# Row factor one step later, four padded buffers, and the neighbourhood and retention tiles scaled by VectorE as it empties their bank

## The reference, cut to what matters

```
h = rms_norm(x, pre_mix_g[l])              # x * row_factor(token) * gain(column)
z = h @ w_in[l]                            # 2048 -> 57 tiles of 128 columns
za, zb, zc = jnp.split(z, [NA_IN_COLS, NA_IN_COLS + RW_IN_COLS], axis=-1)
ya = neighbourhood_attention(...za...)     # 12 tiles
yb = rwkv7_mixer(zb, ...)                  # 21 tiles, token_shift first
yc = retention_mixer(...zc...)             # 24 tiles
x = x + rms_norm(jnp.concatenate([ya, yb, yc], -1) @ w_out[l], post_mix_g[l])
u = jnp.square(jax.nn.relu(rms_norm(x, pre_mlp_g[l]) @ w_up[l])) @ w_down[l]
x = x + rms_norm(u, post_mlp_g[l])
```

## Time and profile before

| | |
|---|---|
| median of 3 runs | 1336.45 us (1335.89 to 1338.19) |
| profiled execution | 1339.37 us, span 1337.6 us, granted clock 0.992 |
| PE busy | 1300.4 us, 97% of the span |
| DVE, ACT, POOL busy | 841.8, 645.5, 329.9 us |
| HBM traffic | 222.56 MB read, 2.10 MB written |

### The profile page before, as it was taken

The page is one execution under the profiler, slowest core; times in us unless marked ns, Lnnn a source line. Parts: engine busy times, 40 slices in busy tenths (PEclk is TensorE's granted clock), DMA queues, the critical chain, the costliest instruction groups (busy, mean ns, idle before and its releaser), DMA issues.

```text
span 1337.6 us, 24793 instructions
## 1 busy us (share of the span) xinstructions
PE 1300.4 (97%) x10204; PEld 1127.1 (84%) x10204; DVE 841.8 (63%) x1151; ACT 645.5 (48%) x991; POOL 329.9 (25%) x273
## 2 busy tenths in 40 slices
PE   9898999999999999999999999999999999999997
PEld 8686888888889898888888888888888888888886
DVE  8767787777775987556555555555554554555564
ACT  7464555565434446457444444444444444444453
POOL 0123234352316231000445555555530000000000
PEclk9899999999999999999999999999999999999999
DMA  9555433223339344782866666666656555565672
GB/s 307 145 159 150 126 106 97 81 81 98 106 107 226 95 127 130 276 274 77 232 181 198 190 188 191 189 190 189 189 189 194 196 194 190 193 197 191 191 235 93
DMA packets 281857, 226.28 MB, mean 169 GB/s; under 512 B 15184, under 2 KB 259024, under 8 KB 281104
## 3 DMA queue, kind: packets, MB, share of 16 engines
q1 hardware_dynamic: 281360, 223.44, 55.4%
q0 software_dynamic: 240, 1.18, 0.3%
q10 hardware_dynamic: 144, 0.07, 0.0%
HBM read 222.56 MB, written 2.10 MB: 168 GB/s over the span
## 4 chain that ended last, share of the span: by engine, by line
PE 65%; DVE 4%; ACT 2%; DMA 2%; issue 1%; DVEq 0%; ACTq 0%
PE psum L2336 30%; PE psum L1917 17%; PE psum L1928 9%; PE psum L1901 2%; PE psum L1907 2%; PE psum L1902 2%; DMA raw<-in_w_out 2%; DVE w_lo L895 1%; ACT w_hi L1490 1%; PE psum L2393 0%; PE psum L2312 0%; DVE arena L1398 0%; PE psum L2214 0%; PE psum L2304 0%; PE psum L2099 0%
## 5 line engine op out<-in xcount | busy, mean ns | idle before, releaser
L895 DVE TENSOR_TENSOR w_lo<-raw,w_hi 128x1024 fp32r<-128x1024 f32 x394 | 500.2, 1272 | 373.7 <-ACT w_hi L1490 370.4
L1490 ACT ACTIVATE w_hi<-raw 128x1024 fp32r<-128x1024 f32 x394 | 417.9, 1064 | 428.4 <-PE psum L2336 186.9
L1917 PE MATMUL psum<-act_both,w_hi 128*128 128x512 f32 x1296 | 319.7, 395 | 9.9 <-ACT w_hi L1490 9.8
L2336 PE MATMUL psum<-w_hi,act_both 128*128 128x512 f32 x1216 | 327.8, 390 | 1.4 <-DVE arena L1319 0.9
L1917 PEld LDWEIGHTS psum<-act_both,w_hi 128*128 128x128 f32 x1296 | 239.3, 190 | 57.3 <-ACT w_hi L1490 10.9
L2336 PEld LDWEIGHTS psum<-w_hi,act_both 128*128 128x128 f32 x1216 | 227.9, 188 | 49.9 <-issue 1.2
L2336 PE MATMUL psum<-w_lo,act_both 128*128 128x512 f32 x608 | 187.6, 389 | 0.0
L1928 PEld LDWEIGHTS psum<-act_both,w_lo 128*128 128x128 f32 x1296 | 170.4, 192 | 8.2 <-DVE w_lo L895 0.3
L1928 PE MATMUL psum<-act_both,w_lo 128*128 128x256 f32 x1296 | 174.2, 283 | 0.0
L1901 PE MATMUL psum<-act_both,w_hi 128*128 128x256 f32 x576 | 157.8, 305 | 0.2 <-ACT w_hi L1490 0.2
L1902 PE MATMUL psum<-act_both,w_hi 128*128 128x256 f32 x576 | 145.7, 284 | 0.0
(11 more groups left out here) (246 smaller groups left out, 1149.8 us busy)
## 6 DMA issues: line engine op xcount, KB each, us to landing
raw<-in_w_up SPq DMA_DIRECT2D x128, 512.0 KB, 4.0
raw<-in_w_down SPq DMA_DIRECT2D x128, 512.0 KB, 3.9
raw<-in_w_in SPq DMA_DIRECT2D x114, 512.0 KB, 4.1
raw<-in_w_out SPq DMA_DIRECT2D x32, 512.0 KB, 4.9
arena<-in_x_t SPq DMA_DIRECT2D x4, 512.0 KB, 7.6
arena<-in_na_rpb SPq DMA_DIRECT2D x16, 128.0 KB, 4.5
arena<-in_x SPq DMA_DIRECT2D x1, 2048.0 KB, 8.7
out_x<-arena SPq DMA_DIRECT2D x3, 512.0 KB, 2.7
```

What stands on the lines that cost most here:

```text
L895: dve.tensor_tensor(by_half(h, low(h)), by_pair(h, raw[:, place[h] % RAW]), by_half(h, high(h)).bitcast(F32), ALU.subtract).then_inc(s["lo ...
L1490: act.activation(by_half(h, high(h)), by_pair(h, raw[:, place[h] % RAW]), ACT.Copy).then_inc(s["hi_half"], 1)
L1917: last = pe.matmul(bank[b], w_hi[:, h % SPLIT, at:at + P], act_both[:, kt].rearrange("p a t -> p (a t)"), start=kt == 0, stop=stop and kt ...
L2336: last = pe.matmul(bank[4 * t + 2 * j + b], lhs[:, tokens], w[:, b * 512:(b + 1) * 512], start=start, stop=stop)
```

## The change

- The gap of the row sum goes from 10 to 11, and root and reciprocal follow at the gaps 12 and 13. The squares of x are added by three 1024-wide additions, one of 512 and one of 256, in place of five reductions; each addition inside the first loop comes one block earlier.
- Four padded buffers in place of two, and larger lags for sum, scale, `to_zs` and shift; the first drains are spread over one gap each. The first turn's preparation starts later, in fewer gaps.
- DVE's `scaled_nr` empties all 18 neighbourhood and retention groups. ACT's `to_nr`, POOL's `scale_na` and POOL's multiplication of the two tables are gone, and what waited for them waits for the drain.

```diff
-SUM_LAG, SCALE_LAG, ZS_LAG, SHIFT_LAG = 3, 4, 9, 13
+SUM_LAG, SCALE_LAG, ZS_LAG, SHIFT_LAG = 11, 12, 20, 28
-NORM_GAP = 10
-ZS_FROM, SHIFT_FROM = 8 * NORM_GAP + 9, 8 * NORM_GAP + 17
+NORM_GAP = 11
+ZS_FROM, SHIFT_FROM = 8 * (NORM_GAP + 5), 8 * (NORM_GAP + 6)
+PADS = 4
...
-        PE_STARTS = {15: "root", 19: "lora"}
-        STARTS = {12: "square", 17: "root", 18: "factor", 20: "norm", 21: "lora", 26: "sums_0", 29: "keys_0",
-                  31: "sums_1", 33: "keys_1"}
+        PE_STARTS = {21: "root", 24: "lora"}
+        STARTS = {19: "square", 22: "root", 23: "factor", 25: "norm", 26: "lora", 29: "sums_0", 32: "keys_0",
+                  34: "sums_1", 36: "keys_1"}
...
-            def scale_na(i):
-
-                pool.wait_ge(s["bank_free"], RW_GROUPS + i + 1)
-                z = cut(nr_at(2 * i), 2, T)
-                pool.tensor_tensor(z, z, row_scale.unsqueeze(1).broadcast_to([P, 2, T]), ALU.mult).then_inc(
-                    s["na_scaled"], 1)
-                pool.wait_ge(s["na_scaled"], i + 1)
...
-            pool.tensor_tensor(turns, turns, row_scale.unsqueeze(1).broadcast_to([P, 2, T]), ALU.mult).then_inc(
-                s["table_scaled"], 1)
...
-                dve.tensor_reduce(x_part[:, q], x_sq[:, q].rearrange("p (k t) -> p t k", t=T), AX_X, ALU.add).then_inc(
-                    s["x_parted"], 1)
+                if q > 1:
+                    dve.wait_ge(s["x_added"], q - 1)
+                dve.tensor_tensor(x_sq[:, 0], x_sq[:, 0], x_sq[:, q], ALU.add).then_inc(s["x_added"], 1)
...
-                dve.tensor_reduce(x_total, x_part.rearrange("p q t -> p t q"), AX_X, ALU.add).then_inc(
-                    s["x_totalled"], 1)
+                dve.wait_ge(s["x_added"], KT // BLOCK_KT - 1)
+                dve.tensor_tensor(x_sq[:, 1, 0:2 * T], x_sq[:, 0, 0:2 * T], x_sq[:, 0, 2 * T:4 * T], ALU.add).then_inc(
+                    s["x_added"], 1)
+                dve.wait_ge(s["x_added"], KT // BLOCK_KT)
+                dve.tensor_tensor(x_total, x_sq[:, 1, 0:T], x_sq[:, 1, T:2 * T], ALU.add).then_inc(s["x_totalled"], 1)
...
                 if q >= 2:
-                    add_squares(q - 2)
+                    add_squares(q - 1)
...
-            at = {"gap": 0, "lo": BLOCK_H, "shift": 0, "sum": 0, "nr": SCALED_FROM}
+            at = {"gap": 0, "lo": BLOCK_H, "shift": 0, "sum": 0, "nr": RW_GROUPS}
...
-                if at["gap"] in (NORM_GAP - 2, NORM_GAP - 1):
-                    add_squares(at["gap"] - NORM_GAP + 4)
-                if at["gap"] == NORM_GAP - 1:
+                if at["gap"] == NORM_GAP - 3:
+                    add_squares(KT // BLOCK_KT - 1)
+                if at["gap"] == NORM_GAP - 2:
                     total_squares()
...
-            def to_nr(g):
-                tiles = group_tiles(g)
-                j = tiles[0] - RW_T
-                act.wait_ge(s["gemm_half"], 2 * (tiles[-1] + 1))
-                if j + 1 >= ZPAD_TILE:
-                    act.wait_ge(s["pad_free"], 2 + RW_GROUPS)
-                act.activation(cut(nr_at(j), 2 * T), bank[6 + g % 2], ACT.Copy).then_inc(s["bank_free"], 1)
...
-                if g < RW_GROUPS:
-                    return max(complete(g) + ZS_LAG, ZS_FROM)
-                return complete(g) + DRAIN_LAG
+                return max(complete(g) + ZS_LAG, ZS_FROM + 8 * g)
...
-            scaled(pe)
+            drained(pe, NA_T - 1)
```

More of the change, by code:

```diff
@@ L715, in tilde @@
                 return [first, nothing, bonus_and_queries, lambda: key_rate(1), nothing, lambda: queries(1), nothing]
-            at = {"gap": 0, "scale": 0, "na": 0}
+            at = {"gap": 0, "scale": 0}
             def scale_z(g):
@@ L855, in _ @@
             dve.memset(eps, EPS).then_inc(s["eps_set"], 1)
-            dve.memset(zpad[:, 0], 0.0).then_inc(s["pad_free"], 1)
-            dve.memset(zpad[:, 1], 0.0).then_inc(s["pad_free"], 1)
+            for n in range(PADS):
+                dve.memset(zpad[:, n], 0.0).then_inc(s["pad_free"], 1)
             dve.memset(all_ones, 1.0).then_inc(s["ones_set"], 1)
@@ L937, in shift @@
                         z = z_of(ct)
[L938 removed]
+                        last = dve.scalar_tensor_tensor(z, zpad[:, g % PADS, j, at:at + T], vect(mu)[:, ct:ct + 1], z,
                                                         ALU.mult, ALU.add)
@@ L944, in shift @@
                 last.then_inc(s["pad_free"], 1)
-            at = {"gap": 0, "lo": BLOCK_H, "shift": 0, "sum": 0, "nr": SCALED_FROM}
+            at = {"gap": 0, "lo": BLOCK_H, "shift": 0, "sum": 0, "nr": RW_GROUPS}
             def gap():
                 done = DONE[at["gap"]]
-                while at["shift"] < RW_GROUPS and max(complete(at["shift"]) + SHIFT_LAG, SHIFT_FROM) <= done:
+                while at["shift"] < RW_GROUPS and max(complete(at["shift"]) + SHIFT_LAG, SHIFT_FROM + 8 * at["shift"]) <= done:
                     shift(at["shift"])
@@ L1506, in to_zs @@
                     ct = RW_ORDER[n]
-                    last = act.activation(z_of(ct), zpad[:, g % 2, j, 1:T + 1], ACT.Copy, scale=small[:, 64 + ct:65 + ct])
+                    last = act.activation(z_of(ct), zpad[:, g % PADS, j, 1:T + 1], ACT.Copy, scale=small[:, 64 + ct:65 + ct])
                 last.then_inc(s["bank_free"], 1)
@@ L1513, in copy_z @@
                 act.wait_ge(s["pad_free"], g + 1)
-                act.activation(zpad[:, g % 2, 0:len(group_tiles(g)), 1:T + 1], rw_halves(g)[:, :, 1], ACT.Copy).then_inc(
+                act.activation(zpad[:, g % PADS, 0:len(group_tiles(g)), 1:T + 1], rw_halves(g)[:, :, 1], ACT.Copy).then_inc(
                     s["z_copied"], 1)
-            def to_nr(g):
-                tiles = group_tiles(g)
-                j = tiles[0] - RW_T
-                act.wait_ge(s["gemm_half"], 2 * (tiles[-1] + 1))
-                if j + 1 >= ZPAD_TILE:
-                    act.wait_ge(s["pad_free"], 2 + RW_GROUPS)
-                act.activation(cut(nr_at(j), 2 * T), bank[6 + g % 2], ACT.Copy).then_inc(s["bank_free"], 1)
             at = {"gap": 0, "hi": BLOCK_H, "copy": 0, "drain": 0}
             def drain_due(g):
-                if g < RW_GROUPS:
-                    return max(complete(g) + ZS_LAG, ZS_FROM)
-                return complete(g) + DRAIN_LAG
+                return max(complete(g) + ZS_LAG, ZS_FROM + 8 * g)
             def gap():
                 done = DONE[at["gap"]]
-                while at["drain"] < SCALED_FROM and drain_due(at["drain"]) <= done:
-                    if at["drain"] < RW_GROUPS:
-                        to_zs(at["drain"])
-                    else:
-                        to_nr(at["drain"])
+                while at["drain"] < RW_GROUPS and drain_due(at["drain"]) <= done:
+                    to_zs(at["drain"])
                     at["drain"] += 1
@@ L1547, in gap @@
                     at["hi"] += 1
-                if at["gap"] == NORM_GAP - 2:
+                if at["gap"] == NORM_GAP - 3:
                     squares(KT // BLOCK_KT - 1)
-                if at["gap"] == NORM_GAP:
+                if at["gap"] == NORM_GAP + 1:
                     row_root()
@@ L1780, in _ @@
                 turn(i)
-            assert at["hi"] == OUT_H + 2 and at["drain"] == SCALED_FROM and at["gap"] == len(DONE) - 1
+            assert at["hi"] == OUT_H + 2 and at["drain"] == RW_GROUPS and at["gap"] == len(DONE) - 1
             gate_heads(RET_CT - 2, RET_CT)
```

40 lines of the change are left out of this document (16 added, 24 removed).

## The result

| | before | changed |
|---|---|---|
| median | 1336.17 us (1333.13 to 1338.19, 4 runs) | 1326.54 us (1324.87 to 1327.22, 4 runs) |
| ratio | | 0.9925, 95% interval 0.9906 to 0.9945 |
| profiled execution | 1339.37 us | 1326.27 us, span 1324.4, granted clock 0.996 |

What follows compares the result with a forecast made beforehand. PE bounds the kernel, busy 97%, so only its idle time and slow stretches can be won. Terms -7.1 - 1.9 - 1.2 + 0 = -10.2 us, from 1336.45 to 1326.2 us; range 1317.5 to 1335.5, own case 1321 to 1331.

Steps and rivals of the forecast that it cites:

- Row sum and first sums: Dense stage: the 2.1 us wait ahead of the row sum moves to half 8; booked 0.
- Behind the row factor: Dense stage, halves behind the row sum: ACT no longer waits for POOL ahead of conversions; -7.1 us, bounds 0 and 7.1.
- for the median I take 1336.45 - 10.2: Final step: the summed gain of 10.2 us subtracted from the median of the runs, giving 1326.2 us.
- Keys: First turn's `keys_0`, `sums_1`, `keys_1` in the dense stage: 6.4 us lost where 8.3 were; -1.9 us.
- First products: Group 9's shifts now stand behind the DVE piece PE waits for, ahead of the first level; -1.2 us, bounds 0 and 2.
- Drains: Product stage: 12 more DVE drains, +2 us uncovered, against -2 for POOL's six multiplications gone; 0, bounds +8.2 and -4.
- the bound of -4: Lower bound of the drains' term in the product stage: at most 4 us won.
- The 1.25 us wait: Wait at 250.98 in the product stage, right behind a POOL multiplication; cited for booking -2 us for POOL's absence.
- PE's waits for DVE in the product stage: Sign that the forecast is right: these waits stay as large as before; doubled would show the second rival.
- the second rival: DVE becomes the product stage's bound, each drain reaching PE in full: 1334.4 us, chance 0.13.

Runs made afterwards that it cites:

- The earlier sum: Changed kernel with only the sums of groups 0 and 9 one gap earlier on DVE: 1323.77 us, ratio 0.9914.
- the drains alone: Kernel before with only DVE's drains of all 18 groups, without the later row factor and the four buffers: 1330.45 us, ratio 0.9965.
- the two edits of the kernel before: Kernel before with ACT's square moved from gap 12 to 16: 1336.03 us; the same with four padded buffers in place of two: 1335.14 us.
- a second drain: Changed kernel with each of the first 12 DVE drains done twice: 1330.62 us, ratio 0.9960.
- the copied drains: Changed kernel with ACT's `to_nr`, POOL's `scale_na` and POOL's table multiplications put back: 1332.21 us, ratio 0.9975.

## Why the prediction was right in sum and wrong in its terms

- *Row sum and first sums, 0.* The mechanism was right, the wait stands at half 8 with 1.84 us for the 2.1 forecast. The booked 0 left out that half 8 then runs slowly: half 11 starts at 43.65 against 42.26, +1.4 us. The earlier sum takes both away.
- *Behind the row factor, -7.1.* That PE waits nowhere there is right: every half from 12 to 20 takes the undisturbed 2.79 us. Between the two profiles the three halves took 15.44 and 8.38 us, so -7.1 to the digit. The step that failed is "for the median I take 1336.45 - 10.2": the loss was measured in one execution that lay 2.9 us above the median, and then subtracted in full from the median. The three other executions with the same order or nearly so lost less; each is one profile. From half 8 to half 16 it was 32.93 us there, 30.57 with the drains alone, 30.25 and 30.30 in the two edits of the kernel before, and 26.71 now. The term with that of the row sum is about -3.7 (26.71 less the mean of the three), not -6.2. The cause named was incomplete too: ACT's 4.30 us for POOL alone costs some 2 to 3; what held up the conversions was a row of pieces (scaling, square, copy, sum behind the shifts). In two edits one of them took over when the one ahead of it went; no run takes all of them away one by one, so their shares stay open.
- *Keys, -1.9.* Right: -2.6, with waits of 0.38, 2.56 and 0.18 us at the halves 34, 36 and 40, where 1.2 and 3.2 were forecast at 34 and 36 and 2.0, hidden, at 38. Against the profile with the drains alone (37.60) it is -1.2.
- *Not booked, +2.1.* With the longer lag the sum of group 9 falls behind DVE's first products, and PE, which needs its bank, waits 1.99 us at 141.63. The prediction looked at the sum of group 0 alone; the same lag moved ten others.
- *First products, -1.2.* Right: from the first matmul behind the dense stage (148.37 before, 141.63 now) to the first products 5.78 and 4.69 us, -1.1. In the turn that follows +1.0 came back: the shift of the last group now stands ahead of a DVE result that PE needs, and PE waits 0.37 and 1.29 us (for L1100 and L1085) where it waited 0.77 once.
- *Drains, 0.* This term hid the most. It booked +2 for uncovered drains and -2 for POOL's absence. The measured sum is -5.2 on the kernel before and -5.4 on the changed one (-4.7 and -6.1 by the ratios), beyond the bound of -4, though the interval of the former, -2.5 to -6.7, reaches it; POOL's six multiplications alone are 4.4 to 5.9. The 1.25 us wait of the earlier trace rows was read as the price of such a collision. Its price was that wait, a second one 27 us later (1.23 at 278.22) and the clock behind them: that turn's mean was 0.93 and it took 47.18 us in place of 42.81. PE's waits for DVE in the product stage, which were to stay as large, fell: those of 0.2 us or more between 147 and 430 us from 6.8 to 4.6 us.

So two errors of about the same size, with opposite signs, met, and that the sum is right is luck: 10.2 us were booked for the parts outside the drains, which by the medians bring about 4 (9.6 in all less the drains' 5.2 to 5.4), some 6 too much, and the drains were booked some 5 too low. The advice of the Trainium skill (Perfetto Trace Analysis, Optimizing Scalar/DVE Operations) that a saturated DVE may be relieved by giving work to ACT, by which the second rival would have been the forecast, did not decide here: a second drain costs PE about half its length, but the first one came with the removal of POOL's multiplications, which is worth more.

## What to carry to other kernels

Ask of an instruction not only what it costs on its own engine but whom it slows while it runs: 12 drains on the busier engine won time because six multiplications on an engine that is three quarters idle stood beside results that PE waits for. Size a stall in more than one execution, or take it off that execution alone: in the third turn the waits came back to 0.1 us with the copied drains (1.25 and 1.23 us, then 1.26 and 1.24), but what the clock cost behind them did not (47.18 us, then 44.53). And when a lag is changed for all groups, look at each place where another engine needs the result: both new waits for sums sat at the groups 0 and 9, behind the block phase and behind half 41, and giving those two their old lag, with group 9's scale and two steps of the preparation moved by a gap, was worth as much again as the whole change.

## What the runs showed that was not expected

Behind waits of the same kind the eight matmuls of half 14 took 3.78 us in the kernel before (idle 3.57) but 2.11 with the drains alone (idle 2.87), where the eight of half 10 had taken 3.26 instead of 2.19. The order is the same; which half pays for a low clock, and for how long, was not the same. Why is left open. Also left open is how much a drain costs PE by itself, since doing it twice measures the second one, and why the executions of the kernel before scatter by 7 to 8 us in each set (17 to 28 executions) and the ten of the changed one by 2.7.
